# Unread products in the opening, and another order of scaling and splitting on VectorE

## The reference

```python
sh1, sc1, g1, sh2, sc2, g2 = jnp.split((silu_c @ ada_w[i] + ada_b[i])[:, None, :], 6, axis=-1)
hl = modulate(rms_norm(x, norm1_g[i]), sh1, sc1)          # h * (1 + scale) + shift
hc = modulate(rms_norm(ctx, norm1_g[i]), csh1, csc1)
yl, yc = diff_attention(hl, hc, diff_w_qkv[j], ...)        # starts with h @ w_qkv, 1024 x 3072
x = x + g1 * yl
hl = modulate(rms_norm(x, norm2_g[i]), sh2, sc2)
y = moe_ffn(...)                                           # 16 experts, 1024 -> 512 -> 1024
```

## Time and profile before

| | us |
|---|---|
| median of 3 runs | 1185.92 (1185.76 to 1186.34) |
| profiled execution | 1186.33 |
| its span | 1184.5 |
| TensorE busy | 989.4 (84% of the span) |
| VectorE busy | 404.9 (34%) |
| ScalarE busy | 374.9 (32%) |
| mean DMA rate | 272 GB/s |

### The profile page before, as it was taken

The page is one execution under the profiler, slowest core; times in us unless marked ns, Lnnn a source line. Parts: engine busy times, 40 slices in busy tenths (PEclk is TensorE's granted clock), DMA queues, the critical chain, the costliest instruction groups (busy, mean ns, idle before and its releaser), DMA issues.

```text
span 1184.5 us, 24437 instructions
## 1 busy us (share of the span) xinstructions
PE 989.4 (84%) x9596; PEld 654.5 (55%) x9597; DVE 404.9 (34%) x809; ACT 374.9 (32%) x803; POOL 218.5 (18%) x329
## 2 busy tenths in 40 slices
PE   3799999978889989799899559999999779886650
PEld 1477777545555666457466447787555546553420
DVE  1533331357833531122122373222854512121103
ACT  3433221466621221122222344233852112221102
POOL 0000000000000024344344201910000224442211
PEclk8799999999989899899899969999999889998775
DMA  9766665998130658999999467224447699999972
GB/s 338 251 214 218 224 217 180 339 362 332 73 155 31 222 221 341 422 420 422 424 422 408 181 217 171 74 71 146 210 124 312 259 399 366 412 423 425 425 310 112
DMA packets 93682, 322.07 MB, mean 272 GB/s; under 512 B 21241, under 2 KB 33954, under 8 KB 81330
## 3 DMA queue, kind: packets, MB, share of 16 engines
q1 hardware_dynamic: 85746, 305.40, 66.7%
q0 software_dynamic: 7008, 12.62, 2.9%
q10 hardware_dynamic: 864, 3.15, 0.7%
HBM read 313.67 MB, written 13.99 MB: 277 GB/s over the span
## 4 chain that ended last, share of the span: by engine, by line
PE 65%; DMA 17%; DVE 7%; issue 4%; SPq 3%; ACT 2%; POOL 1%; DVEq 0%; POOLq 0%; ACTq 0%
PE ps L1878 24%; PE ps L1643 20%; DMA expert_sets<-in_moe_w_up_dram 10%; PE ps L1794 7%; PE ps L1546 4%; DMA ada_late<-in_ada_w_dram 3%; PE ps L1570 2%; DMA ring<-in_diff_w_qkv_dram 2%; SPq L608 1%; PE ps L1723 1%; PE ps L1752 1%; PE ps L1696 1%; SPq L590 1%; PE ps L1849 1%; DMA expert_rows<-moe,scatter_idx 1%
## 5 line engine op out<-in xcount | busy, mean ns | idle before, releaser
L1878 PE MATMUL ps<-expert_sets,moe 128*32 128x256 f32 x6304 | 369.9, 397 | 77.8 <-DMA expert_sets<-in_moe_w_up_dram 45.4
L1878 PEld LDWEIGHTS ps<-expert_sets,moe 128*32 128x32 f32 x6304 | 234.1, 115 | 212.9 <-issue 101.4
L1504 DVE STREAM_TRANSPOSE moe<-moe 128x256 f32<-128x256 f32 x70 | 46.0, 657 | 313.3 <-PE ps L1878 294.8
L1643 PE MATMUL ps<-w_high,x_high 128*128 128x512 f32 x352 | 143.5, 408 | 7.3 <-DVE hT L506 2.7
L1643 PE MATMUL ps<-w_high,x_low 128*128 128x512 f32 x352 | 139.8, 397 | 0.0
L1643 PE MATMUL ps<-w_low,x_high 128*128 128x512 f32 x352 | 139.6, 397 | 0.0
L473 DVE TENSOR_TENSOR w_low<-ring,w_high 128x2048 fp32r<-128x2048 f32 x24 | 58.0, 2424 | 131.4 <-ACT w_high L470 131.4
L743 POOL MEMSET moe<- 128x128 f32 x2 | 0.4, 206 | 548.6 <-PE ps L1820 548.6
L1068 ACT ACTIVATE moe<-ps 128x128 f32<-128x128 f32 x68 | 18.9, 278 | 259.7 <-PE ps L1878 257.5
L766 POOL DMA_INDIRECT expert_rows<-moe,scatter_idx x74 | 75.9, 1026 | 77.3 <-POOL scatter_idx L803 56.1
L1643 PEld LDWEIGHTS ps<-w_high,x_high 128*128 128x128 f32 x352 | 67.8, 192 | 32.0 <-issue 17.3
(11 more groups left out here) (235 smaller groups left out, 1118.9 us busy)
## 6 DMA issues: line engine op xcount, KB each, us to landing
expert_sets<-in_moe_w_down_dram SPq DMA_DIRECT2D x32, 2048.0 KB, 20.3
expert_sets<-in_moe_w_gate_dram SPq DMA_DIRECT2D x30, 2048.0 KB, 16.2
expert_sets<-in_moe_w_up_dram SPq DMA_DIRECT2D x30, 2048.0 KB, 21.2
ring<-in_ada_w_dram SPq DMA_DIRECT2D x16, 2048.0 KB, 8.0
ring<-in_diff_w_qkv_dram SPq DMA_DIRECT2D x6, 2048.0 KB, 8.1
ada_late<-in_ada_w_dram SPq DMA_DIRECT2D x6, 2048.0 KB, 11.8
ring<-in_na_w_qkv_dram SPq DMA_DIRECT2D x6, 2048.0 KB, 9.0
rows<-mod_rows SPq DMA_DIRECT2D x12, 512.0 KB, 8.6
```

The lines of the kernel that those rows point to most:

```text
L1504: dve.transpose(blk_inT, blk_in[b].rearrange("p (j k) -> p k j", k=KC)).then_inc(m_xt[l], 1)
L1643: mm = pe.matmul(ps[:, n % 2], x_part[:, k, tok], w_part, start=(k == 0 and i == 0), stop=(k == KC - 1 and i == 2))
L1878: mm = pe.matmul(ps[g * SLOTS:(g + 1) * SLOTS, bank, 0:n_out], lhs_T[:, k, :], weights(k, g), start=(k == 0), stop=(k == n_chunks - 1), sk ...
```

## The change

On TensorE, `keep_busy` moves up to the opening, and 8 unread products are put ahead of the third modulation strip's products and 3 ahead of the fourth's. On VectorE, `stream_in` scales both of its pairs first and then makes the two halves of x_low; on ScalarE the order stays. The second part holds for all four calls of `stream_in`, two in each layer.

```diff
@@ -504,7 +504,11 @@
                         eng.activation(dst, src, ACT.Identity, bias=shift, scale=scale).then_inc(s_heA[l], 1)
                     else:
                         eng.tensor_scalar(dst, src, scale, shift, ALU.mult, ALU.add).then_inc(s_heD[l], 1)
-                split_inputs(eng, l, s, half)
+                if eng is nc.scalar:
+                    split_inputs(eng, l, s, half)
+            if eng is nc.vector:
+                for half in range(2):
+                    split_inputs(eng, l, s, half)
@@ -1581,7 +1585,13 @@
+            def keep_busy(count):
+
+                for _ in range(count):
+                    pe.matmul(ps[:, 3, 0:2 * P], ident, cst[:, 0:2 * P], start=True, stop=True)
+
             for a in range(ADA_QKV):
+                keep_busy((0, 0, 8, 3)[a])
                 mod_products(a)
                 mod_turn(a)
@@ -1843,11 +1853,6 @@
-                def keep_busy(count):
-
-                    for _ in range(count):
-                        pe.matmul(ps[:, 3, 0:2 * P], ident, cst[:, 0:2 * P], start=True, stop=True)
-
                 keep_busy((19, 13)[l])
```

## The result

The changed kernel takes 1190.17 us, median of 7 executions (1186.98 to 1193.14), against 1186.34 (7 executions, 1184.68 to 1187.80) for the kernel before on the same chip: a ratio of 1.0030 with an interval of 1.0015 to 1.0044. It is slower by 3.6 us where 2.2 us less was forecast, and the time lies outside the range. The profiled execution took 1186.98, span 1185.0, and was the fastest of its seven.

The account below looks back on a forecast made before the run. TensorE's projection products bound the kernel, started late by a VectorE-ScalarE wait chain in the opening. 0 + 1.29 + 0.7 + 0.2 = 2.2 us off the 1185.92 median gave 1183.7; 8-in-10 range 1181.4 to 1186.2.

Parts of the forecast that it names:

- part 1's price: Opening, TensorE's 8 + 3 unread products: costed at 0, since ScalarE's w_high cast waits for its strip's transfer anyway.
- the rival of a low clock: Opening: unread products run at the low clock and delay the cast to 40.1; 1187.0 us, chance 0.09.
- wrong if the cast starts later than 38.9: Opening, ScalarE's cast of w_high: forecast at 38.5, as before; a start after 38.9 would refute the prediction.
- The bound of 0.4 lost: Opening, DMA: next modulation strip's load, issued about 1.7 us earlier, overlaps the projection strip; put at 0, at worst 0.4 lost.
- a rival of the prediction: Opening: w_high cast later from that load's overlap, or gain lost at a later engine; 1.0 or more lost, 1185.2, chance 0.14.
- about 1.85: Opening, TensorE: fourth modulation strip's products at the high clock take about 1.85 us instead of 3.57.
- 1.7 was worked out: Opening: modulation ready some 1.7 us sooner, so VectorE's first pair could start at 37.6 instead of 39.39.
- the slower rival: The low-clock case: unread products at the low clock, cast of w_high at 40.1; 1187.0 us, chance 0.09.
- 1.29 in the opening: Opening: VectorE's second pair moved ahead lets x_high's second half start at 43.43, not 44.72; first product at 48.08, 1.29 us gained.
- 0.2 in the second layer: Second layer's stream_in: VectorE's order brings TensorE's first product to 696.8 from 697.08; 0.2 us taken, bounds -0.5 and 0.3.
- The clock's 0.7: Opening, first job of 24 products: earlier turning may bring the clock's rise forward; 0.7 us taken, between 0 and 2.41.
- A later part could absorb it: Expert blocks, partly fed by DMA, might absorb the gain; dismissed because their loads, issued as TensorE frees buffers, also come forward.

Follow-up runs that it names:

- e1: Kernel before with only VectorE's new order in stream_in, no unread products added in the opening: 0.9978 of the kernel before, 1184.77 us.
- e14: Repeat of e1, VectorE's order alone, on one chip with the changed kernel: 0.9981 of the kernel before, 1183.26 us.
- e12: The changed kernel measured again, unaltered, in a later comparison: 1.0024 of the kernel before, 1189.74 us.
- e3: Kernel before plus 11 tiny unread 32x32 products behind the program's first two turns, adding 44 instruction words: 1.0047 of the kernel before.
- e8: Changed kernel plus 53 tiny 32x32 products behind the first two turns, 256 added words in all: 1.0009 of the kernel before, 1186.59 us.
- e9: Kernel before plus 11 tiny 32x32 products between the layers, moving only the second layer's code by 44 words: 1.0015 of the kernel before.
- e10: e1 with layer 0's router unread products made wider and 11 fewer, so later code stands 44 words earlier: 1.0000 of the kernel before.
- e5: Kernel before plus 64 tiny 32x32 products behind the first two turns, 256 added words: 1.0011 of the kernel before.
- e6: Kernel before plus 32 tiny 32x32 products behind the first two turns, 128 added words: 1.0073 of the kernel before.
- e7: Kernel before plus 48 tiny 32x32 products behind the first two turns, 192 added words: 1.0051 of the kernel before.
- e4: Changed kernel with layer 0's router unread products wider and 11 fewer, putting later code back in place: 0.9988 of the kernel before, 1187.50 us.
- e2: Kernel before with only the 8 + 3 unread products added in the opening, VectorE's order old: 1.0042 of the kernel before.
- e11: e1 plus 11 tiny 32x32 products behind the first two turns, adding 44 words: 1.0006 of the kernel before.

## Why the prediction was wrong

**The step that failed is part 1's price.** It read: "It adds 8 + 3 fp32 products of 128x256 on TensorE and nothing else", and "I cost part 1 at 0", with 1.7 gained and 0.4 lost as bounds beside the rival of a low clock. Beside its work it adds 44 words ahead of everything that TensorE runs later. Measured, part 1 costs the changed kernel 1.0030 - 0.9978 = 0.0052 or, on one chip, 1.0024 - 0.9981 = 0.0043: 5.1 to 6.2 us. Two places make it up:
- in the expert blocks, 26.7 and 26.9 us of issue waits against e1's 21.8 and e14's 22.3: 4.4 to 5.1;
- in the opening, the first product at 48.69 (49.04 in e12) with part 1 and at 47.91 (e1) or 47.82 (e14) without: 0.8 to 1.2.

That sums to 5.2 to 6.3. It is an estimate, for idle time of single executions is added up as if all of it reached the end: behind 1060 us TensorE waits for expert weights (10.75 us at 1100.1 in the changed kernel, 8.95 at 1100.0 before), and these loads, issued when it frees buffers, carry the delay on. That the position is the cause of the first is shown by e3 to e8; that waits for code are how it works is the reading that fits the rows.

**The opening loss has the same source.** The prediction was "wrong if the cast starts later than 38.9", and it starts at 39.19. The DMA view of the changed kernel, 0 to 38 us, has one row that the kernel before has not:

```profile
q8 instruction: 1, 0.02, 0.2%
```

The first instruction packet comes at 36.7, ahead of the projection strip's landing; before it came at 52.5. In the ten other kernels with words added in the opening it comes between 12.5 and 37.2, and their casts start at 39.38 to 39.71; in the four others (e1, e9, e10, e14), packet at 46.8 or later, at 38.32 to 38.45. Fourteen experiments divide that way without exception.

The delay also starts where the packet comes. In the four kernels whose first packet precedes the third modulation strip's landing (e5, e6, e7, e8: 12.5 to 26.7), that strip's products already start at 28.6 to 29.0; in the twelve others at 27.2 to 27.8. The third strip and the projection strip are late where a packet came before their landing, and only there.

How 16 KB hold a 2 MB strip back is not shown, but an estimate fits in size: the packet of 36.7 has 3.4% of the 16 DMA engines' time between 36 and 38, which is 1.1 us of one engine. If each strip is spread over all of them and has landed when the last is done, it lands up to that much later; 0.6 to 1.2 against the kernel before was measured.

The bound of 0.4 lost stood for this landing, with another cause, the next modulation strip's load, issued earlier than 37.18; a rival of the prediction rested on the same. That cause is excluded: in e9 the load is issued at 35.02 and the cast starts at 38.44, in e4 and e6 it is issued at 37.75 and 38.40 and the cast starts at 39.38 and 39.71.

**Hidden work was hidden, but not always at the high clock.** In the first profile the rest of part 1 came out as written: clock 1.00 at 24 and where the strips' products stand, these in 1.92 against "about 1.85", nothing gained by them, because ScalarE waits for its strip; VectorE's first pair starts 2.4 us sooner, where 1.7 was worked out. In the second profile of the same kernel, e12's, the clock fell to 0.50 at 28.7. The three unread products took 2.77 us instead of 1.46, and they stand in its chain of waits (start, duration, what held it):

```profile
31.76 2.56 PE ps L1591 x6
34.32 2.52 PE ps L1574 x16
```

It fell at 28.4 in e2 and at 25.9 in e4 too, with the same 2.8 us for the three. So part of the slower rival's mechanism does happen. It cost nothing: from the cast of w_high to the first product it is 9.49 in e12 and 9.50 in e4, as in the first profile, and 10.80 in e2, which has the old order, as before. The rival's sign came true by another mechanism.

**Part 2 was right in its mechanism.** 1.29 in the opening: 1.31 measured from cast to first product. 0.2 in the second layer: the chain of the changed kernel there is

```profile
689.55 3.66 PE ps L1550 x16
...
693.23 1.00 DVE hT L506 x2
694.23 1.14 DVE x_low L486
...
695.62 12.76 PE ps L1653 x48
```

From first turn to first product it is 6.07; before it was 697.08 - 690.70 = 6.38 (the earlier trace rows and the prediction's 697.08). 0.3 gained. Alone it measured 2.6 and 2.3 us against a forecast of 2.2, but that nearness is partly luck: the intervals of these two reach from 0.7 to 4.3 us, and 0.7 of the forecast is the clock's, which the next paragraph takes away. The opening and the second layer give 1.6; where the rest came from is not shown.

**The clock's 0.7 has no evidence.** The changed kernel's first job took 5.68 in one profile and 7.39 in e12's; the kernel before 7.88; e1 8.12 and e14, the same program, 6.27; e9, in which the opening is the old one, 5.72. In 8 of the 16 profiles the clock is at 1.00 before the first product, and the job takes 5.68 to 5.73; four of the eight have the old order, of seven such profiles, and four the new one, of nine. So the rise comes early or late by execution, and no effect of the order on it shows. The prediction put 0.7 because the executions it knew lay within 0.6 us, "which does not look like a clock that one run gets early and another late"; in the comparison of e9 to e11 the kernel before alone spans 1181.75 to 1192.87. The changed kernel's first profile had the early rise, so 2.2 of its lead of 2.9 is that luck. Nor does the clock carry the loss: over the executions of e12's comparison the changed kernel had a mean granted clock of 0.933 against 0.926 for the kernel before, and was slower.

**"A later part could absorb it"** was named and dismissed. The lead of the first profile was lost there, and with it the gain, for the most part where the waits with fetches stand; the prediction had thought of waits for data alone, and dismissed it because the loads come forward too. In e1 and e14, whose code stands where it stood, the lead lasts to the end (4.1 and 4.5 us at 1180).

What stays open: which branch meets which block; why e4 and e8 keep 0.1% and more of the loss against e1 (their first product, 1.0 us later than e1's, would be 0.08%; in its profile e4 loses 3.3 us from 930 to 1000, with its code back in place); and that the waits, summed from one execution each, follow the time closely but not exactly (e5 24.5 at 1.0011, e10 24.5 at 1.0000).

## What to carry to other kernels

Where an engine's program has loops and branches behind a straight part, an added instruction is not free even where its time is: before an edit is judged by its mechanism, compare it with a kernel in which instructions of the same number do nothing, and measure the position on its own with a few paddings, up to a whole block of 256. Padding that keeps later code in place, or a whole block of it, lets a change be judged for what it does. And price an edit's parts apart: here a good one of 0.2% was hidden by one priced at nothing that cost 0.4% to 0.5%.

## What the runs showed of the hardware

- Moving TensorE's code by products that do next to nothing goes with up to 0.73% (32 tiny products), 8.7 us in 1186, and with 0.11% after 256 words.
- An instruction packet of 16 KB on its way ahead of a 2 MB strip goes with a landing 0.6 to 1.2 us later than in the kernel before, in all 11 kernels that have one.
- The clock can rise behind turning alone: in the changed kernel TensorE had only turned for 3.65 us from 44.37, then waited 0.67, and the clock was 1.00 from 48.1, ahead of the first product at 48.69. In e1, with the same turning, it was still 0.50 to 52.6, so turning can end in the rise and need not. The rule that the prediction weighed ("TensorE: Matmul & The Clock Gate", Part 4: PE-mode transpose, of the Trainium skill) says that transposes do not open the high clock; this row speaks against it, if these turns, which the profile lists as MATMUL, are in the mode that the page means, which no trace here shows.
